# Three more seven-product pairs and shorter head turns in a hybrid decoder block

## The reference

```python
q, k, v, cb, cc, ch, g_conv, g_attn = jnp.split(einsum('bsd,de->bse', x, w_in[l]), SPLIT_POINTS)
y_conv = cb * causal_conv3(cc * ch, conv_w)
y_attn = sliding_window_attention(q, k, v, sinks)      # 16 heads of 64, 4 KV heads, window 128, ALiBi
merged = sigmoid(g_conv) * y_conv + sigmoid(g_attn) * y_attn
x = layer_norm(ALPHA * x + einsum('bse,ed->bsd', merged, w_out[l]), ln1_g[l], ln1_b[l])
hid = silu(x @ w_gate) * (x @ w_up)
x = layer_norm(ALPHA * x + hid @ w_down, ln2_g[l], ln2_b[l])
```

## Time and profile before

| what | value |
|---|---|
| median of 3 runs | 1350.9 us (1350.8 to 1351.47) |
| the profiled execution | 1350.05 us |
| its span, first to last instruction | 1347.8 us |
| PE busy | 1336.1 us, 99% |
| DVE, ACT, POOL busy | 827.2, 527.1, 721.8 us |
| chain that ended last | PE lines for the most part |

### The profile page before, as it was taken

How to read it: one execution, slowest core, us unless ns; L and a number is a source line. 1 busy time by engine, 2 the same in 40 slices (tenths; PEclk the granted TensorE clock), 3 DMA queues, 4 the chain that set the end, 5 groups by cost and what they waited for, 6 DMA issues and landing times. The chain is left out here.

```text
span 1347.8 us, 18068 instructions
## 1 busy us (share of the span) xinstructions
PE 1336.1 (99%) x6506; PEld 1174.3 (87%) x6506; DVE 827.2 (61%) x1151; ACT 527.1 (39%) x973; POOL 721.8 (54%) x487
## 2 busy tenths in 40 slices
PE   9999999999999999999999999999999999999997
PEld 8888888888888888888888888888888888888886
DVE  5656555576867768677578664535545455464547
ACT  6432322335565564755444332232322323223133
POOL 5578887721222121235881875573755737566374
PEclk9999999999999999999999999999999999999999
DMA  8311222211111111123620221211112112121113
GB/s 250 119 51 53 60 63 63 58 52 48 32 33 47 48 32 32 47 82 107 186 79 1 79 63 49 70 57 44 62 47 70 54 39 70 47 68 50 47 55 125
DMA packets 133199, 88.96 MB, mean 66 GB/s; under 512 B 9104, under 2 KB 123792, under 8 KB 133136
## 3 DMA queue, kind: packets, MB, share of 16 engines
q1 hardware_dynamic: 133136, 88.12, 21.5%
HBM read 79.72 MB, written 8.39 MB: 65 GB/s over the span
## 5 line engine op out<-in xcount | busy, mean ns | idle before, releaser
L848 POOL TENSOR_TENSOR w_lo<-raw,w_hi 128x512 fp32r<-128x512 f32 x80 | 110.3, 1379 | 204.2 <-ACT w_hi L1222 204.2
L693 POOL TENSOR_TENSOR w_lo<-raw,w_hi 128x1024 fp32r<-128x1024 f32 x28 | 67.9, 2424 | 219.9 <-ACT w_hi L907 209.9
L1680 DVE TENSOR_TENSOR res<-res,ps 128x512 f32<-128x512 f32 x128 | 87.2, 686 | 60.1 <-PE ps L1851 60.1
L1849 PE MATMUL ps<-hid_hi,wd_hi 128*128 128x512 f32 x320 | 121.5, 380 | 0.1
L1850 PE MATMUL ps<-hid_lo,wd_hi 128*128 128x512 f32 x320 | 121.3, 379 | 0.0
L1851 PE MATMUL ps<-hid_hi,wd_lo 128*128 128x512 f32 x320 | 121.3, 379 | 0.0
L2147 PE MATMUL ps<-act_hi,w_hi 128*128 128x512 f32 x320 | 121.3, 379 | 0.0
L2148 PE MATMUL ps<-act_lo,w_hi 128*128 128x512 f32 x320 | 121.3, 379 | 0.0
L2149 PE MATMUL ps<-act_hi,w_lo 128*128 128x512 f32 x320 | 121.3, 379 | 0.0
L1849 PE MATMUL ps<-act_hi,w_hi 128*128 128x512 f32 x272 | 104.5, 384 | 0.0
L1850 PE MATMUL ps<-act_lo,w_hi 128*128 128x512 f32 x272 | 103.1, 379 | 0.0
(11 more groups left out here) (261 smaller groups left out, 3558.0 us busy)
## 6 DMA issues: line engine op xcount, KB each, us to landing
raw<-in_w_in SPq DMA_DIRECT2D x28, 512.0 KB, 3.8
raw<-in_w_in SPq DMA_DIRECT2D x48, 256.0 KB, 3.0
raw<-in_w_gate SPq DMA_DIRECT2D x40, 256.0 KB, 2.8
raw<-in_w_up SPq DMA_DIRECT2D x40, 256.0 KB, 3.1
raw_d<-in_w_down SPq DMA_DIRECT2D x20, 512.0 KB, 3.4
raw<-in_w_out SPq DMA_DIRECT2D x16, 512.0 KB, 4.0
xs<-in_x SPq DMA_DIRECT2D x8, 512.0 KB, 7.1
x_channels<-res SPq DMA_DIRECT2D x2, 2048.0 KB, 7.9
```

The source lines that it names most:

```text
L848: pool.tensor_tensor(wide(ring(w_lo, n)), src, fp(wide(ring(w_hi, n))), ALU.subtract).then_inc(pl_s, 1)
L1680: dve.tensor_tensor(tile, tile, bank, ALU.add).then_inc(add_s, 1)
L1849: pe.matmul(bank, w_h(t), hi, start=(t == 0), stop=False)
```

## The change

`PLAIN` becomes `(3,)`. Turns 0 to 2 lose their gc and cb units and become short (8 units, 8 steps per block); the three pairs (gc, cb, 1), (gc, cb, 3) and (gc, cb, 5) join the conv stage, which then has 15 pairs. As 105 products end in another weight slot than 84 did, head tiles before the last turn's gc tile use the other `w_hi`/`w_lo` slot (`head_slot`), and the last turn's second pair of ga units is swapped. The division is shared: DVE divides two heads, ACT the other two (`divide`, with the semaphore `share_s`). The due times of several steps in short blocks change: on ACT, `turn` and the unit drains come ahead of the next exponents; on PE `turn` comes at 9 instead of 11, and `values` at 16.05, right behind the scores of the block after next. Low parts of most q units on DVE come 5.5 steps after the unit instead of 0.9. In the output stage `channel_sum(0, 5)` is placed behind `out_low_part(8)`, the first mixer parts come 4 steps later, and the variance and spread steps one step of three matmuls later.

```diff
-PLAIN = (0, 1, 2, 3)
+PLAIN = (3,)
...
-    UNITS += [(_i, 0), (_i + 1, 0), (_i, 1), (_i + 1, 1)]
+    UNITS += [(_i, 0), (_i + 1, 0)] + ([(_i + 1, 1), (_i, 1)] if _k in PLAIN else [(_i, 1), (_i + 1, 1)])
...
+SAME_SLOTS = HEAD_TILES.index((PLAIN[0], "gc", 1))
+def head_slot(t):
+    return (t + 1) % 2 if t < SAME_SLOTS else t % 2
+def before_in_slot(t):
+    return t - 2 if t < SAME_SLOTS or t >= SAME_SLOTS + 2 else 2 * SAME_SLOTS - 1 - t
...
-PE_STEPS = sorted([(block_at(b, 0), "scores", b) for b in BLOCKS] + [(block_at(b, 14, 11), "turn", b) for b in BLOCKS]
-                  + [(block_at(b, 20, 15), "values", b) for b in BLOCKS])
+PE_STEPS = sorted([(block_at(b, 0), "scores", b) for b in BLOCKS] + [(block_at(b, 14, 9), "turn", b) for b in BLOCKS]
+                  + [(block_at(b, 20, 16.05), "values", b) for b in BLOCKS])
+def low_later(u):
+    tile, h = UNITS[u]
+    k, kind, j = HEAD_TILES[tile]
+    if kind == "q" and 0 < unit_end(u) <= LAST_TURN:
+        return 1.5 if (j, h) == (1, 0) else 5.5
+    return 0.2 if kind == "cb" else 0.9
 ACT_STEPS = scheduled(
...
-    [(block_at(b, 4.3), "exp", b) for b in BLOCKS],
-    [(block_at(b, 15.2, 12.1), "turn", b) for b in BLOCKS],
-    [(block_at(b, 21.2, 16.1), "values", b) for b in BLOCKS],
+    [(block_at(b, 4.3, 3.6), "exp", b) for b in BLOCKS],
+    [(block_at(b, 8.4, 6.4), "divide", b) for b in BLOCKS],
+    [(block_at(b, 15.2, 9.5), "turn", b) for b in BLOCKS],
+    [(block_at(b, 21.2, 16.15), "values", b) for b in BLOCKS],
...
-    [(LAST_TURN + 14 + 4 * m, "mix_first", m) for m in range(6)],
+    [(LAST_TURN + 18 + 4 * m, "mix_first", m) for m in range(6)],
...
 DVE_STEPS = scheduled(
...
-    [(block_at(b, 8.2, 7.5), "exp", b) for b in BLOCKS],
-    [(block_at(b, 16.2, 13), "turn", b) for b in BLOCKS],
-    [(block_at(b, 22.2, 17.2), "values", b) for b in BLOCKS],
+    [(block_at(b, 8.2, 6.3), "exp", b) for b in BLOCKS],
+    [(block_at(b, 16.2, 12), "turn", b) for b in BLOCKS],
+    [(block_at(b, 22.2, 19), "values", b) for b in BLOCKS],
...
-    [(out_end(m) + 2, "channel_sum", m) for m in range(6)])
+    [(out_end(m) + 2, "channel_sum", m) for m in range(5)])
...
             out_low_part(8)
+            channel_sum(0, 5)
             out_low_part(9)
...
+            def divide(b):
+                lo = P if b % NB == 0 else 0
+                act.wait_ge(soft_s, SOFT * b + 3)
+                for g in (2, 3):
+                    act.activation(prob[:, g, lo:], prob[:, g, lo:], ACT.Copy,
+                                   scale=rden[:, g:g + 1]).then_inc(share_s, 1)
...
             def normalise(b):
                 lo = P if b % NB == 0 else 0
                 dve.wait_ge(exp_s, G * (b + 1))
+                if b:
+                    dve.wait_ge(share_s, 2 * b)
                 dve.reciprocal(rden[:], rsum[:]).then_inc(soft_s, 1)
                 soft_done(b, 3)
-                dve.tensor_tensor(prob[:, :, lo:], prob[:, :, lo:],
-                                  rden[:].rearrange("p (g o) -> p g o", o=1).broadcast_to([P, G, 2 * P - lo]),
+                dve.tensor_tensor(prob[:, :2, lo:], prob[:, :2, lo:],
+                                  rden[:, :2].rearrange("p (g o) -> p g o", o=1).broadcast_to([P, 2, 2 * P - lo]),
                                   ALU.mult).then_inc(soft_s, 1)
...
             def turn_probs(b):
                 k, n = b // NB, b % NB
                 pe.wait_ge(soft_s, SOFT * b + SOFT)
+                pe.wait_ge(share_s, 2 * b + 2)
...
-                                   DT + 3: {2: lambda: variance(0), 5: lambda: spread(0)}}.get(v, {}))
+                                   DT + 3: {3: lambda: variance(0), 6: lambda: spread(0)}}.get(v, {}))
```

More of the change, by code:

```diff
@@ L140 @@
     [(-40, "weight", 0), (-33, "weight", 1)],
-    [(unit_end(last_unit(t - 2)) + 0.2, "weight", t) for t in range(2, len(HEAD_TILES))],
+    [(unit_end(last_unit(before_in_slot(t))) + 0.2, "weight", t) for t in range(2, len(HEAD_TILES))],
     [(unit_end(last_unit(len(HEAD_TILES) - 2 + v)) + 0.2, "out_weight", v) for v in range(2)],
     [(out_end(v - 2) + 0.2, "out_weight", v) for v in range(2, DT)],
-    [(block_at(b, 4.3), "exp", b) for b in BLOCKS],
-    [(block_at(b, 15.2, 12.1), "turn", b) for b in BLOCKS],
-    [(block_at(b, 21.2, 16.1), "values", b) for b in BLOCKS],
-    [(-30 if k == 0 else block_at(NB * k - 6, 8.1), "keys", k) for k in range(NKV)],
-    [(-31 if k == 0 else block_at(NB * k - 7, 8.1), "value_rows", k) for k in range(NKV)],
-    [(LAST_TURN + 14 + 4 * m, "mix_first", m) for m in range(6)],
+    [(block_at(b, 4.3, 3.6), "exp", b) for b in BLOCKS],
+    [(block_at(b, 8.4, 6.4), "divide", b) for b in BLOCKS],
+    [(block_at(b, 15.2, 9.5), "turn", b) for b in BLOCKS],
+    [(block_at(b, 21.2, 16.15), "values", b) for b in BLOCKS],
+    [(-30 if k == 0 else block_at(NB * k - 6, 8.1, 6.5), "keys", k) for k in range(NKV)],
+    [(-31 if k == 0 else block_at(NB * k - 7, 8.1, 6.5), "value_rows", k) for k in range(NKV)],
+    [(LAST_TURN + 18 + 4 * m, "mix_first", m) for m in range(6)],
     [(LAST_TURN + 63.8, "mix_first", m) for m in (6, 7)],
@@ L155 @@
 DVE_STEPS = scheduled(
-    [(unit_end(u) + (0.2 if HEAD_TILES[UNITS[u][0]][1] == "cb" else 0.9), "unit", u) for u in range(len(UNITS))
+    [(unit_end(u) + low_later(u), "unit", u) for u in range(len(UNITS))
      if HEAD_TILES[UNITS[u][0]][1] != "ga"],
     [(block_at(b, 1), "scores", b) for b in BLOCKS],
-    [(block_at(b, 8.2, 7.5), "exp", b) for b in BLOCKS],
-    [(block_at(b, 16.2, 13), "turn", b) for b in BLOCKS],
-    [(block_at(b, 22.2, 17.2), "values", b) for b in BLOCKS],
+    [(block_at(b, 8.2, 6.3), "exp", b) for b in BLOCKS],
+    [(block_at(b, 16.2, 12), "turn", b) for b in BLOCKS],
+    [(block_at(b, 22.2, 19), "values", b) for b in BLOCKS],
     [(-29 if k == 0 else block_at(NB * k - 6, 4.6, 4.1), "value_rows", k) for k in range(NKV)],
@@ L167 @@
     [(-27 if k == 0 else block_at(NB * k - 1, 8.5, 7.7), "sink", k) for k in range(NKV)],
-    [(LAST_TURN + 14.8 + 4 * m, "mix_first", m) for m in range(6)],
+    [(LAST_TURN + 18.8 + 4 * m, "mix_first", m) for m in range(6)],
     [(LAST_TURN + 64.6, "mix_first", m) for m in (6, 7)],
@@ L176 @@
     [(-39, "weight", 0), (-32, "weight", 1)],
-    [(unit_end(last_unit(t - 2)) + 1.5, "weight", t) for t in range(2, len(HEAD_TILES))],
+    [(unit_end(last_unit(before_in_slot(t))) + 1.5, "weight", t) for t in range(2, len(HEAD_TILES))],
     [(unit_end(last_unit(len(HEAD_TILES) - 2 + v)) + 1.5, "out_weight", v) for v in range(2)],
@@ L362, in build @@
         x_kept, x_sum0 = sem("x_second_half_kept"), sem("x_first_half_sum")
+        share_s = sem("softmax_divided_on_act")
         xf_s, xf_hi_s, xf_lo_s = sem("x_form"), sem("x_form_hi"), sem("x_form_lo")
@@ L690, in _, with low_part @@
                                pattern=[[1, 2 * P]], channel_multiplier=-1).then_inc(tables, 1)
-            def low_part(count, slot):
+            def low_part(count, slot, raw_slot=None):
                 pool.wait_ge(w_hi_s, count)
-                pool.tensor_tensor(w_lo[:, slot], raw[:, slot], fp(w_hi[:, slot]), ALU.subtract).then_inc(w_lo_s, 1)
+                pool.tensor_tensor(w_lo[:, slot], raw[:, slot if raw_slot is None else raw_slot], fp(w_hi[:, slot]),
+                                   ALU.subtract).then_inc(w_lo_s, 1)
             pool.wait_ge(w_first_s, 1)
@@ L792, in _ @@
                 if step == "weight":
-                    low_part(PRO_TILES + n + 1, n % 2)
+                    low_part(PRO_TILES + n + 1, head_slot(n), n % 2)
                 elif step == "merge_first":
@@ L902, in _, with high_part @@
         def _(act):
-            def high_part(landed, slot, free, count):
-                act.wait_ge(w_in_s[slot], landed)
+            def high_part(landed, slot, free, count, raw_slot=None):
+                raw_slot = slot if raw_slot is None else raw_slot
+                act.wait_ge(w_in_s[raw_slot], landed)
                 if free is not None:
                     act.wait_ge(free, count)
-                act.activation(w_hi[:, slot], raw[:, slot], ACT.Copy).then_inc(w_hi_s, 1)
+                act.activation(w_hi[:, slot], raw[:, raw_slot], ACT.Copy).then_inc(w_hi_s, 1)
             def x_high(i):
@@ L1004, in head_weight @@
                 if t < 2:
-                    free, count = c_prod, max(n + 1 for n in range(7 * NCP) if n % 4 // 2 == t)
+                    free, count = c_prod, max(n + 1 for n in range(7 * NCP) if n % 4 // 2 == head_slot(t))
                 else:
-                    free, count = unit_s, 2 * PRO_TILES + last_unit(t - 2) + 1
-                high_part(16 * ((PRO_TILES + t) // 2 + 1), t % 2, free, count)
+                    free, count = unit_s, 2 * PRO_TILES + last_unit(before_in_slot(t)) + 1
+                high_part(16 * ((PRO_TILES + t) // 2 + 1), head_slot(t), free, count, t % 2)
             def head_unit(u):
@@ L1118, in _ @@
                     exponents(n)
```

(4 more changed lines are left out.)

## The result

The changed kernel takes 1355.64 us (median of 6 runs, 1355.21 to 1356.41) where the kernel before took 1350.87 beside it (6 runs, 1350.8 to 1351.5): a ratio of 1.0035, interval 1.0025 to 1.0045. It is slower by 0.35%, or 4.8 us, where the forecast was 0.6 us more than before: 1351.5, with a range of 1342 to 1356. The result lies inside that range by 0.4 us. The profiled execution took 1355.49 us, with a span of 1353.7, which is 5.9 more than before.

The account below looks back on a forecast made before the run. PE's matmul count at 0.216 us each bounds it, while helpers deliver in time. 1350.05 - 8.4 (removed matmuls, output stage) + 9.0 (stalls in three turns) = 1350.65; the median lies 0.85 above: 1351.5 us, range 1342 to 1356.

Parts of the forecast that it names:

- Removed matmuls: Three pairs moved to the conv stage, 96 matmuls becoming 84 in each: 7.77 us of PE saved, no wait there.
- rival 4: Conv stage: a 0.3 us wait in each of 15 pairs, or no saving from the pairs; 1356 us, chance 0.03.
- Output stage: Output stage: the gap at unit 8 goes and the squares' wait stays in absolute time, together -0.65 us.
- The mechanism at unit 8: Output stage: POOL does low part 8 before channel sum 5, so PE's unit 8 loses its 0.69 us gap.
- my walk: Turn 1, reciprocal to reciprocal through blocks 3 to 7: 34.58 us with locks, giving 3.0 us of PE stall per turn.
- locks forecast at blocks 4, 5 and 7: Short turns: POOL's operations delay DVE's gate (block 4, 1.1 us), bias (block 5, 1.2) and gate (block 7, 1.8).
- Rival 2: Block 7: DVE wins the last race with POOL, stall 1.2 us per turn; 1346.1 us, chance 0.20.
- rival 1: Short turns: gates and keys miss POOL's operations, so there is no stall; 1342.5 us, chance 0.20.
- ending 0.28 behind it: Every DVE operation with two SBUF inputs begun inside a POOL operation ends 0.28 us after that operation.
- the gate begins at 4.6 as POOL does, and I give it to DVE: Block 3: DVE's gate and POOL's low part start together 4.6 us into the block, and DVE is first.
- rival 3: Block 3: POOL wins the race, reciprocal 11 is 1.25 us late, stall 4.2 per turn; 1355.2 us, chance 0.17.
- Block 16 has half the work and DVE catches up: Next turn's first block: with half the work there, DVE makes up its lateness after a 3.0 us stall per turn.

Follow-up runs that it names:

- e1: The kernel before with only the output-stage edits and the first mixer parts 4 steps later: 1350.18 us, ratio 0.9997 to the kernel before.
- e9: The changed kernel with one added wait, POOL's low parts in short turns waiting for their block's gate: 1346.58 us, ratio 0.9969 to the kernel before.
- e6: The changed kernel with short-turn weight tiles rounded first, keys' high parts a block earlier, value rows and both bias pairs in block 2: 1340.73 us, ratio 0.9927.
- e2: The changed kernel with POOL writing zeros (memset) instead of subtracting for low parts of head tiles 2 to 13: 1345.3 us, ratio 0.9961.
- e7: e6 with the division of all four heads back on DVE: 1352.48 us, ratio 1.0011 to the kernel before.
- e10: e9 with the division of all four heads back on DVE: 1353.23 us, ratio 1.0014 to the kernel before.

## Why the prediction was right and wrong

- **Removed matmuls**: -7.77 and no wait in the conv stage, as forecast; rival 4 is out.
- **Output stage**: -0.65 forecast, -1.26 in the one execution, but e1 could not tell the edits from nothing. The mechanism at unit 8 is as described; what it is worth stays open.
- **Forms on DVE and ACT**: from one reciprocal to the next in turn 1 my walk had 8.16, 9.23, 8.03 and 9.16; the trace has 8.36, 9.45, 8.23 and 9.19 (447.98 to 456.34, and so on to 483.21), 0.65 us more in all. From the division to the scaled scores it takes 0.82 us (448.18 to 449.00) where I had 0.72, and the o_sum pair takes 1.04 where I had 0.98. ACT's share is 0.91 where I took 0.8. These terms were too small: in turn 0 PE has lost 3.7 us (0.36 + 1.37 + 0.36 + 1.59) when it gets probabilities 15, instead of 3.0. That is 0.7 a turn, 2 us over the kernel.
- **Shared access**: the locks forecast at blocks 4, 5 and 7 all came (1.0, 1.2 and 1.6 us against 1.1, 1.2 and 1.8). Rival 2, the last lock falling to DVE, did not happen in any turn, nor did rival 1. The rule "ending 0.28 behind it" was too wide: it holds for the gate and for one bias, but the keys ended 1.08 us after POOL. The walk had given the keys 1.1 all the same, so the sum is not hurt. e9 shows that the lock is the cause: with the gates out of POOL's way, stalls fall by 9 us with no work removed, and in e6, where order alone is changed, 1.2 of the 16.0 us are left. By the Trainium skill (SBUF — State Buffer, "Who interferes with whom") a VectorE instruction with two SBUF inputs contends with a GpSimd instruction that reads SBUF, and not with one that only writes it. These runs agree: the gate took up to 2.65 us beside the subtraction, and 0.43 beside e2's memset.
- **The step that failed, first**: "the gate begins at 4.6 as POOL does, and I give it to DVE". In turns 0 and 2 DVE did win (its gate kept 0.42 us, and POOL's low part took 2.64 and 2.57). In turn 1 POOL was first by 0.07 us. That is rival 3, in one turn of three: turn 1 loses 1.2 us more than turn 0 and 0.9 more than turn 2, and I had priced it at 1.25.
- **The step that failed, second, and the larger one**: "Block 16 has half the work and DVE catches up". The walk ended with probabilities 15, and so did not look at the gate and POOL's next low part in block 16. They start together (487.07), and the gate takes 2.65. From reciprocal 15 to reciprocal 16 it takes 9.19 us (483.21 to 492.40), as long as with a full block, 2.2 of them by this lock; without it, by this sum, DVE would have caught up. PE loses another 1.1 us behind it, in all three turns: 3.4 us. In turns 0 and 1 they lie in the next B1; in turn 2, before the longer blocks of the last turn, they are in the 2.76 of B0.

Together: 9.0 forecast, + 2 for small terms, + 1.2 for block 3, + 3.4 for block 16 is 15.6 of the 16.0 measured. The mechanism was right, and so were most of its meetings; the stalls were forecast at little more than half.

The time hides part of this. The stalls are 7.0 us above the forecast, the time only 4.1. The profiled execution's first conv product came 1.1 us earlier, by no effect of the change; the output stage was 0.6 shorter than forecast; and the rest is the distance between the profiled executions and the medians. So that the time lies within the range, by 0.4 us, is in part luck. Rival 3's time, 1355.2, is near the 1355.6 measured by luck too: it has 12.7 us of stalls and not 16.0, and its race came in one turn of three.

Sharing the division helps by itself, but it also moves the gate into the first tenths of POOL's operation, where a lock costs most. A gate that comes 1.2 us into it loses 1.0, one that comes with it 2.2.

## What to carry to other kernels

When two engines lock each other out, the order of two starts less than 0.1 us apart can cost 2 us; walk every meeting of the two through the turn's seam, not only up to the last wait that you look for. Then take the meetings apart by order, not by speed: put the blocking operation beside work that it doesn't touch (here DVE's operations with at most one SBUF input), and move the rest out of its way (e6), which turned +0.35% into -0.73%. Where an experiment makes the victim slower and the kernel faster, suspect a race, and repeat it with the race removed before judging the part.

## What the runs showed of the hardware

- A DVE operation with two SBUF inputs that begins inside a POOL subtraction ends after it by about its own length less 0.14 us: the gate (0.43 alone) 0.28 after, the keys' low part and the full division (1.22 alone) 1.08 after. So it loses what is left of POOL's operation at its start, less 0.14: 2.2 us for a gate of 2.65 (the changed kernel), 1.95 for a division of 3.17 (e7), 1.0 for keys of 2.20 (e9).
- Where the DVE operation is first, it keeps its length and POOL's grows: 2.64 instead of 2.37 us beside a gate that began 0.03 us before it.
- Beside POOL's memset of the same tile the gate kept 0.43 (e2). DVE operations with at most one input in SBUF (the scaling, the minimum and the sum from PSUM) kept 1.23, 1.22 and 1.00 us beside POOL's subtraction (e6).
- Which engine comes first can be decided by less than 0.1 us. In the one trace of the changed kernel POOL was first at the next turn's first block in all three turns alike (gates of 2.63, 2.65 and 2.64 us), but at block 3 in turn 1 alone.
- Pauses of PE of up to 1.2 us left the granted clock at 1.00 in the changed kernel's head stage. Behind pauses of 2.0 us (e10) and 2.3 us (e7) it fell to the 1.2 GHz level, with matmuls 0.43 us apart. Behind a pause of 1.3 us and 16 matmuls of one column in the output stage (e1) the clock was 0.60 over 4 us.
- A copy with a scale per partition of 128x256 takes 501 ns on ACT, two in a row 0.91 us (the changed kernel).
